# Heads' stage: six sums of squares, placed in twos between the parts of the projection's third tile

## The reference, cut to what matters

```python
qkv = jax.nn.silu(depthwise_conv_centred(qkv, conv_w))          # 5 taps along the tokens
q, k, v = jnp.split(qkv, [QK_WIDTH, 2 * QK_WIDTH], axis=-1)
q = l2_normalize(q.reshape(bsz, seq_len, N_HEADS, HEAD_DK).astype(jnp.float32)) * (HEAD_DK ** -0.5)
k = l2_normalize(k.reshape(bsz, seq_len, N_HEADS, HEAD_DK).astype(jnp.float32))
v = v.reshape(bsz, seq_len, N_HEADS, HEAD_DV).astype(jnp.float32)
def l2_normalize(x):
    return x * lax.rsqrt(jnp.sum(x * x, axis=-1, keepdims=True) + NORM_EPS)
```

## Time and profile before

| | us |
|---|---|
| median of 3 runs | 4025.66 (4021.17 to 4031.53) |
| the profiled execution's own time | 4022.98 |
| its span | 4020.8 |
| PE busy over the span | 3379.4 (84%) |
| DVE busy | 1561.8 (39%) |
| ACT busy | 1038.0 (26%) |
| the heads' stage, first product to the barrier behind it | 1858.96 to 2193.7 |
| one head in it | 41.0 |

### The profile page before, as it was taken

The page is one execution under the profiler, slowest core; times in us unless marked ns, Lnnn a source line. Parts: engine busy times, 40 slices in busy tenths (PEclk is TensorE's granted clock), DMA queues, the critical chain, the costliest instruction groups (busy, mean ns, idle before and its releaser), DMA issues. The chain is left out here.

```text
span 4020.8 us, 80592 instructions
## 1 busy us (share of the span) xinstructions
PE 3379.4 (84%) x33244; PEld 2818.0 (70%) x33244; DVE 1561.8 (39%) x2569; ACT 1038.0 (26%) x2010; POOL 377.0 (9%) x407
## 2 busy tenths in 40 slices
PE   7989988888878869998997599999958994978881
PEld 5867777788757759997887488888858873544440
DVE  3145653344236542114665345555434424111113
ACT  2022221122132220012444144455422111211111
POOL 0000000000000010000000122233110000222221
PEclk9989999999989979999999699999978996999896
DMA  3334546211234432333443311111014337999995
GB/s 105 94 101 165 173 166 206 92 50 50 76 144 153 136 105 84 95 91 123 155 153 126 101 32 39 38 49 38 24 47 139 122 93 289 418 419 417 413 400 189
DMA packets 315075, 594.03 MB, mean 148 GB/s; under 512 B 57489, under 2 KB 222202, under 8 KB 285830
## 3 DMA queue, kind: packets, MB, share of 16 engines
q1 hardware_dynamic: 265289, 460.83, 32.4%
q10 hardware_dynamic: 38628, 112.71, 8.2%
q0 software_dynamic: 10928, 17.08, 1.2%
HBM read 471.32 MB, written 139.97 MB: 152 GB/s over the span
## 5 line engine op out<-in xcount | busy, mean ns | idle before, releaser
L3150 PE MATMUL ex_bank_ps<-ex_w_gate_up_sb,ex_xT_sb 128*64 128x256 f32 x2240 | 298.3, 424 | 83.5 <-DMA ex_w_gate_up_sb<-in_w_up_e 79.9
L361 PE MATMUL in_bank_ps<-in_h_hi_sb,in_w_hi_sb 128*128 128x352 f32 (+4 forms) x968 | 333.8, 345 | 10.7 <-DVE in_w_lo_sb L316 10.7
L361 PE MATMUL in_bank_ps<-in_h_lo_sb,in_w_hi_sb 128*128 128x352 f32 (+4 forms) x968 | 331.2, 342 | 0.0
L361 PE MATMUL in_bank_ps<-in_h_hi_sb,in_w_lo_sb 128*128 128x352 f32 (+4 forms) x968 | 330.6, 342 | 0.0
L3150 PEld LDWEIGHTS ex_bank_ps<-ex_w_gate_up_sb,ex_xT_sb 128*64 128x64 f32 x2240 | 174.7, 148 | 215.3 <-issue 124.7
L1483 PE MATMUL mix_bank_ps<-mix_y_hi_sb,mix_wb_hi_sb 128*128 128x512 f32 (+2 forms) x480 | 171.1, 356 | 70.3 <-DVE mix_y_lo_sb L1674 54.8
L433 PE MATMUL qkv_tile_bank_ps<-in_h_hi_sb,qkv_tile_w_hi_sb 128*128 128x352 f32 (+1 forms) x576 | 188.2, 327 | 11.8 <-DVE qkv_tile_w_lo_sb L420 11.8
L361 PEld LDWEIGHTS in_bank_ps<-in_h_hi_sb,in_w_hi_sb 128*128 128x128 f32 (+1 forms) x968 | 180.7, 187 | 24.3 <-issue 11.4
L3338 DVE TENSOR_TENSOR ex_hidden_sb<-ex_silu_g_sb,ex_bank_ps 128x128 f32<-128x128 f32 x70 | 20.2, 288 | 450.8 <-ACT ex_silu_g_sb L3202 444.8
L361 PEld LDWEIGHTS in_bank_ps<-in_h_hi_sb,in_w_lo_sb 128*128 128x128 f32 (+1 forms) x968 | 180.9, 187 | 14.7
L361 PEld LDWEIGHTS in_bank_ps<-in_h_lo_sb,in_w_hi_sb 128*128 128x128 f32 (+1 forms) x968 | 180.9, 187 | 13.5
(11 more groups left out here) (460 smaller groups left out, 7701.7 us busy)
## 6 DMA issues: line engine op xcount, KB each, us to landing
ex_w_gate_up_sb<-in_w_gate_e SPq DMA_DIRECT2D x70, 1024.0 KB
ex_w_gate_up_sb<-in_w_up_e SPq DMA_DIRECT2D x70, 1024.0 KB
ex_w_down_sb<-in_w_down_e SPq DMA_DIRECT2D x70, 1024.0 KB
in_w_sb<-in_w_in SPq DMA_DIRECT2D x45, 512.0 KB, 4.3
scr_p2T<-in_o_sb ACTq DMA_DIRECT2D x28, 520.0 KB
qkv_x_sb<-scr_p2T SPq DMA_DIRECT2D x8, 1560.0 KB, 7.0
scr_p2T<-qkv_tile_o_sb ACTq DMA_DIRECT2D x24, 520.0 KB
prep_tile_w_sb<-in_w_in SPq DMA_DIRECT2D x24, 512.0 KB
```

Of the source, the lines that this page charges most:

```text
L361: last = pe.matmul(bank[:width, 4 * s + n, 0:m], w_[:, s, k, 0:width], h_[:, k, a:a + m], start=(k == 0 and z == 0), stop=(k == KT - 1 and ...
L3150: last = t.matmul(bank[m * BT:(m + 1) * BT, GU_B + b % 2, 0:2 * P], xT[:, s, k, at:at + BT], wgu[:, ws, :, k, m::M], start=(k == 0), stop= ...
```

## The change

`product` takes a function `between`, which it calls behind each part of a tile but the last. Of the three products of a head, the first two stay as they were. Behind the second, PE waits for the squares and issues sums 0 and 1. Sums 2 and 3 are issued behind the first part of the third tile, and sums 4 and 5 behind its second part. The waits between sums and `Ln` are the same. Nothing is changed on the other engines.

```diff
-    def product(self, pe, i, u):
+    def product(self, pe, i, u, between=None):
...
                     last = pe.matmul(self.bank[:, s, n, 0:m], w_[:, s, k, :], h_[:, k, a:a + m],
                                      start=(k == 0 and z == 0), stop=(k == KT - 1 and z == 2))
+            if between and n < len(self.pcs) - 1:
+                between(n)
         last.then_inc(self.mm_done, 1)
...
-                    for n in range(TPH):
-                        tiles.product(t, g, TPH * u + n)
-
-                        if n != 1:
-                            continue
-                        ac.wait(t, h, "square", 1)
-                        for j, (q, c) in enumerate(sums):
+
+                    def head_sums(js):
+                        for j in js:
+                            q, c = sums[j]
 
                             if j >= 2:
                                 ac.wait(t, h, "ln", *sums[j - 2])
...
+                    for n in range(TPH - 1):
+                        tiles.product(t, g, TPH * u + n)
+                    ac.wait(t, h, "square", 1)
+                    head_sums((0, 1))
+                    tiles.product(t, g, TPH * u + TPH - 1, between=lambda c: head_sums((2 * c + 2, 2 * c + 3)))
+                    assert len(sums) == 2 * len(pcs) == 6
```

## The result

The changed kernel takes 4041.16 us (median of 6 runs, 4035.66 to 4049.82) against 4024.52 (6 runs, 4019.41 to 4031.53) before. The ratio is 1.0042, with a 95% interval of 1.0027 to 1.0057: slower by 11 to 23 us. The forecast was 4048.5, its range 4031 to 4057, with 0.77 on slower by over 0.3%.

A forecast was written before the change was run, and what follows sets the result against it. PE was taken to bound the stage. Later head starts 6.7, the clock's fall 15.8 and the stage's end 3 made 25.5 us on top of 4022.98, so 4048.5 us, range 4031 to 4057.

The forecast's parts named there:

- its gap in the sums: PE's wait for an Ln inside each head's sums; removing it was to save PE 2.9 us a head.
- The handover between a sum and a tile: PE's passage from a sum to tile matmuls; taken as 0, other bound 0.25 us at each of two handovers.
- the chain through the outs: From last Ln through table load, Exp and DVE's outs to the next head's weight split; 4.7 us later, against 4.0 slack.
- The loss per head: The next head's first tile on PE starts 0.95 us later, 6.7 us over 7 passages between heads.
- The gap makes the clock fall: PE's new gap of about 3.6 us before the next head drops its clock: 15.8 us over 7 gaps.
- The estimate by the example of the Trainium skill: Alternative price for PE's clock loss: 0.83 us per gap, 5.8 us in all, giving 4038.5 us.
- The end of the stage: In the last head the later stores and third tile's copy lengthen the stage by 3 us, between 1.7 and 4.7.
- the later start: The term for the next head's first tile starting late on PE: 6.7 us over 7 passages.
- The steady clock: Rival: PE's new gap leaves the clock alone, adding 9.7 us, so 4032.7 us; chance 0.15.
- The faster rival: Rival: the weight split is not late, so PE's 23 us less 3 are won, 4003 us; chance 0.05.
- The third, no change: Rival: PE's saved gap and the longer chain cancel, 4023 us; chance 0.03.

The follow-up runs named there:

- e1: The changed kernel with DVE's split of the next head's first weight tile moved ahead of the outs; 3994.93 us, ratio 0.9921 to the kernel before.
- e5: The changed kernel with each pair of sums one part earlier and ACT's roots ahead of the second tile's copy; 3997.53 us, ratio 0.9929 to before.
- e2: The changed kernel with 6 unread float32 matmuls per head added behind the third tile to fill PE's gap; 4029.41 us, ratio 1.0009 to before.
- e6: The changed kernel with 2 unread matmuls per head added behind the third tile, leaving a shorter PE gap; 4032.44 us in one run.
- e4: The changed kernel run again without any edit, in a second set; 4049.09 us, ratio 1.0058 to the kernel before.

## Why the prediction was right, and what was off

*PE bounds the stage, and its gap in the sums is worth 2.9 us a head.* Right, and a little more. In e1 and e5 a head takes 37.85 where it took 41.0: 3.1. The handover between a sum and a tile, which I had priced at 0 with 0.25 as the bound, costs nothing: two sums take 1.18 (1922.51 - 0.16 - 1921.17).

*The moved sums lengthen the chain through the outs by 4.7, and PE then waits for the split.* Right. The last `Ln` came at T+11.96 for T+12.15, the split at T+18.64 for T+18.85. The loss per head was put at 0.95. In e2, where the clock holds, and in the heads of e6 without a fall, the first tiles lie 41.7 us apart, so it is **0.7 to 0.75**, and 5 us over seven passages for 6.7. e1 shows that it is this wait: with the split moved it is gone, and PE keeps all that it saved.

*The gap makes the clock fall, 2.25 us a head.* Right in kind, short in size. All seven gaps, 3.6 to 3.7 us long, were followed by the low clock. The head behind the first took 43.33 us, 1.6 more than 41.7, the next five 2.65 more each. The last fall lies in the stage's last head, behind which no head starts; it is taken as equal, since its slow records last 5.7 us too. That is 17.5 in all, where the sum had 15.8, and e2 gives 17.2. I had taken the mean of three lengths. In this kernel the long stretch of 5.7 us came back behind each gap but the first. The estimate by the example of the Trainium skill ("TensorE: Matmul & The Clock Gate", "HAM oscillation — how this bites in real kernels"), 0.83 us per gap, would have been a third of it; that the clock goes down behind such waits, the trace bears out.

*The end of the stage, 3 us.* e2's 7.7 less the 5 of the passages leaves 2.7, and the changed kernel's 24.9 - 5 - 17.5 leaves 2.4. So 3 was about right in size, but not for the reason of its upper bound. From the store of k I had read 7.0 us or more to its landing. In the changed kernel the stage ended 6.1 us behind the issue of that store (2206.34 to 2212.46), so it took less. The last store to be issued was the third tile's, 4.0 us before the barrier. Its copy on ACT stands behind the heads' stores and started 4.9 us behind the start of the last tile matmul (2202.24 to 2207.15), where it had been 0.35.

*Sum.* 25.5 us against 24.9 in the profiled stage, and 25.0 in e4. That the sum is nearer than its terms is luck: the clock was 1.7 too low, the later start 1.7 too high. The medians of the whole time gave 16.6 and 24.7. The forecast for the time, 4048.5, is therefore 7 us above the first set and at the second. The stage, read in one execution of each set, came out as forecast; the 8 us between the sets were not in it. I had not asked how much of a single execution's time is chance; my range was made from the stage's terms alone.

*The rivals.* The steady clock fell with the profile, and e2 shows what it would have given: +7.7 us in the stage, for 9.7. The faster rival was wrong as a forecast. Its price was right, though: it named 20 us, and with the split out of the way (e1) the stage gains 19.4, with the roots early enough (e5), where the longer end falls away too, 25. The third, no change, fell with the interval of the ratio, which lies above 1 in both sets.

## What to carry to other kernels

Work that fills one engine's gap is late for whoever reads it. Follow its reader's chain to the first instruction that the filled engine itself waits for, on every engine's program order, before counting the gap as won. Here one weight split, whose inputs were there, stood behind two instructions that waited for the roots, and taking it out from behind them, or making them early, turned a loss of 25 us in the stage into a gain of 19 to 25. On PE a new gap of a few microseconds has to be priced with the clock behind it, which here cost over three times what the later start did (17 us against 5).

## What the runs showed that I had not expected

The clock's fall does not follow the gap's length alone. Gaps of 2.4 to 2.5 us let it fall 3 times in 7 (e6), while the heads' gaps of 2.5 to 2.6 us in the kernel before did so in none of its profiles. That both happen could have been read ahead of the prediction, in a later stage of the same trace, with other work around the gaps. Of two gaps there as long as those in the heads, both waits for a load of weights, one was followed by the low clock and one was not. On PE's timeline, and by the view of busy time for what follows each:

```profile
3599.65 4.53 PE L3150 MATMUL ex_bank_ps<-ex_w_gate_up_sb,ex_xT_sb 128*64 128x256 f32 x24 [2.53 <-DMA ex_w_gate_up_sb<-in_w_up_e]
...
3847.88 3.85 PE L3150 MATMUL ex_bank_ps<-ex_w_gate_up_sb,ex_xT_sb 128*64 128x256 f32 x32 [2.61 <-DMA ex_w_gate_up_sb<-in_w_up_e]
```

```profile
3599.70:3603.70 4.00, 4.00 (x22) 2.38 (x24) 0.00 (x0) 0.00 (x0) 0.19 (x1) 0.57 1.02 423
3847.90:3853.00 5.10, 5.10 (x44) 3.43 (x46) 0.50 (x3) 0.28 (x1) 0.97 (x2) 1.00 1.01 422
```

Of the gaps in that stage that began at full clock, 4 of the 7 of 2.0 to 3.0 us let it fall, in the gap or within 1.5 us behind it, and all 11 of 3.0 to 5.0 us did. So the trace bore out the fall behind gaps of 3.6 us with more rows than the prediction's three, and it had rows against the belief that 2.6 us do no harm.

Nor does it always fall within the gap. Behind six of the changed kernel's gaps the first matmul was already slow. Behind the first PE ran at full pace for 1.4 us and then slowly until 1901.45:

```profile
1896.88 0.32 PE L433 MATMUL qkv_tile_bank_ps<-in_h_lo_sb,qkv_tile_w_hi_sb 128*128 128x352 f32 x1
...
1898.23 0.49 PE L433 MATMUL qkv_tile_bank_ps<-in_h_hi_sb,qkv_tile_w_hi_sb 128*128 128x352 f32 x1
...
1901.45 0.34 PE L433 MATMUL qkv_tile_bank_ps<-in_h_hi_sb,qkv_tile_w_lo_sb 128*128 128x352 f32 x1
```

And the loss repeated itself: five heads in a row of the changed kernel took 44.3 to 44.4 us, and the same in e4. What sets where the fall begins was not tried.
